# The first half of an output projection spread over six attention heads of a two-layer encoder

## What is computed

```python
for l in range(DEPTH):                                   # 2 layers
    u = rmsnorm(h, norm_g[l])
    p = u @ w_in[l]                                      # 1024 x 9216
    hq, hf_f, hf_b, hi, hgt, aq, ak, av, agt = jnp.split(p, split_idx, axis=-1)
    o_h = hgrn2_mixer(hq, hf_f, hf_b, hi, hgt, lbs[l], hg_norm_g[l])       # 8 heads
    o_a = diff_attention_mixer(aq, ak, av, agt, diff_lambda[l], diff_subln_g[l], l, cos, sin)
    mixed = jnp.concatenate([o_h, o_a], axis=-1)
    h = h + mixed @ w_out[l]                             # 2048 x 1024
out = rmsnorm(h, final_norm_g)[:, N_META:]
```

## Time and profile before

| what | value |
|---|---|
| median of 3 runs | 1385.91 us (1385.78 to 1386.55) |
| the profiled execution's own time | 1386.22 us |
| its span from first to last instruction | 1384.4 us |
| granted TensorE clock | 0.999 of 2.4 GHz |
| PE busy | 1369.9 us (99%) |
| DVE, ACT, POOL busy | 1046.2, 837.3, 186.0 us |

### The profile page before, as it was taken

The page is one execution under the profiler, slowest core; times in us unless marked ns, Lnnn a source line. Parts: engine busy times, 40 slices in busy tenths (PEclk is TensorE's granted clock), DMA queues, the critical chain, the costliest instruction groups (busy, mean ns, idle before and its releaser), DMA issues.

```text
span 1384.4 us, 32303 instructions
## 1 busy us (share of the span) xinstructions
PE 1369.9 (99%) x13108; PEld 1291.0 (93%) x13108; DVE 1046.2 (76%) x1765; ACT 837.3 (60%) x1802; POOL 186.0 (13%) x158
## 2 busy tenths in 40 slices
PE   9999999999999999999999999999999999999998
PEld 9999999998999999999998888888888899999987
DVE  6888887788646777877667888888886478888864
ACT  7666666666434666666555667666664456666654
POOL 1111222220000000000001122222210000000100
PEclk9999999999999999999999999999999999999999
DMA  5332322332323333333233232333323233334432
GB/s 188 117 98 93 108 85 86 108 108 78 99 71 122 101 99 100 103 90 100 70 107 108 87 106 85 108 107 108 108 82 108 85 110 107 108 107 114 114 96 76
DMA packets 76340, 140.41 MB, mean 101 GB/s; under 512 B 9504, under 2 KB 39456, under 8 KB 76192
## 3 DMA queue, kind: packets, MB, share of 16 engines
q1 hardware_dynamic: 76192, 138.35, 33.0%
HBM read 112.36 MB, written 17.30 MB: 94 GB/s over the span
## 4 chain that ended last, share of the span: by engine, by line
PE 89%; DVE 5%; ACT 2%; issue 2%; DMA 0%; SPq 0%; DVEq 0%; ACTq 0%
PE proj L1926 64%; PE far L2191 5%; PE pair L2174 3%; PE pair L2176 3%; PE far L2208 2%; PE pair L2059 1%; PE far L2193 1%; PE far L2144 1%; PE far L2145 1%; PE pair L2124 1%; DVE ops L1660 1%; PE pair L1926 1%; PE pair L2131 1%; DVE w_lo L1392 1%; PE far L2148 1%
## 5 line engine op out<-in xcount | busy, mean ns | idle before, releaser
L1926 PE MATMUL proj<-u_hi,w_hi 128*128 128x264 f32 (+1 forms) x1960 | 478.7, 312 | 1.9 <-DVE w_lo L1392 0.7
L1926 PE MATMUL proj<-u_lo,w_hi 128*128 128x264 f32 (+1 forms) x1960 | 458.2, 302 | 0.0
L1926 PE MATMUL proj<-u_hi,w_lo 128*128 128x264 f32 (+1 forms) x1960 | 458.1, 302 | 0.0
L1926 PEld LDWEIGHTS proj<-u_hi,w_hi 128*128 128x128 f32 x1960 | 314.7, 189 | 19.3 <-issue 1.4
L1926 PEld LDWEIGHTS proj<-u_hi,w_lo 128*128 128x128 f32 x1960 | 314.0, 188 | 13.6
L1926 PEld LDWEIGHTS proj<-u_lo,w_hi 128*128 128x128 f32 x1960 | 314.0, 188 | 10.6
L1392 DVE TENSOR_TENSOR w_lo<-w_raw,w_hi 128x1024 fp32r<-128x1024 f32 x178 | 221.9, 1247 | 35.9 <-ACT w_hi L952 35.8
L1200 ACT ACTIVATE decay<-pair,neg_max 128x528 f32<-128x528 f32 (+1 forms) x144 | 100.3, 697 | 203.4 <-DVE neg_max L1782 203.3
L952 ACT ACTIVATE w_hi<-w_raw 128x1024 fp32r<-128x1024 f32 x178 | 186.5, 1048 | 39.4 <-PE proj L1926 36.6
L1782 DVE TENSOR_REDUCE neg_max<-pair 128x1 f32<-128x528 f32 (+1 forms) x144 | 101.4, 704 | 90.5 <-PE pair L2176 89.3
L892 POOL TENSOR_TENSOR mix_lo<-mixed_t,mix_hi 128x528 fp32r<-128x528 f32 (+1 forms) x32 | 50.9, 1590 | 502.0 <-ACT mix_hi L1247 502.0
(11 more groups left out here) (257 smaller groups left out, 2245.7 us busy)
## 6 DMA issues: line engine op xcount, KB each, us to landing
w_raw<-w_units SPq DMA_DIRECT2D x178, 512.0 KB, 3.6
v_scratch<-blocks SPq DMA_DIRECT2D x128, 64.0 KB, 2.1
v_rows<-v_scratch SPq DMA_DIRECT2D x32, 256.0 KB, 2.9
o_scratch<-blocks SPq DMA_DIRECT2D x104, 64.0 KB, 2.7
q_stack<-gate_f SPq DMA_DIRECT2D x32, 132.0 KB, 2.4
k_stack<-k_stack SPq DMA_DIRECT2D x32, 132.0 KB, 2.4
o_rows<-o_scratch SPq DMA_DIRECT2D x14, 256.0 KB, 3.8
ops<-o_scratch SPq DMA_DIRECT2D x12, 256.0 KB, 2.6
```

Source lines behind the costliest of these rows:

```text
L1926: ins = pe.matmul(out, w, x[:, tile, cols_n], start=(k == 0 and p == 0), stop=(k == last_k and p == 2))
```

## The change

Four things are done together.

1. The eight `outA` units no longer all hang on head 8. Heads 8 to 13 feed 2, 1, 1, 2, 1 and 1 of them (`OUT_A_BEHIND`), and parts are carried over from head to head (`CARRIED`). Heads 8 to 13 now feed 41, 42, 41, 43, 42 and 43 pieces; heads 14 and 15 stay at 32 and 28.
2. Since the slots of `mix_hi` and `mix_lo` are then read until head 13's end, the outputs of heads 8 to 13 are kept unrounded in six rows of `ops` (free in the attention heads). All are rounded in head 14: ACT in steps 1 to 5 and 7, POOL as they come.
3. Head 7 also feeds the first four pieces of head 9's `aq` unit (`AHEAD`): 39 instead of 35.
4. Special offsets of head 8 (an earlier `av`, a later `ak`, an earlier `ag`, weight parts cut ahead of the step's own work) go.

```diff
+KEPT = range(HG_HEADS, HEADS - 2)
+OUT_A_BEHIND = dict(zip((c + 1 for c in KEPT), (2, 1, 1, 2, 1, 1)))
...
-        if c == HG_HEADS + 1:
-
-            units += [("outA", c, j, c - 1) for j in range(OUT_TILES)]
+        for _ in range(OUT_A_BEHIND.get(c, 0)):
+            units.append(("outA", c, sum(u[0] == "outA" for u in units), c - 1))
...
-def mix_step(c):
-
-    return HG_STEPS - 2 if c < HG_HEADS else 2 if c == HG_HEADS else gate_step(c) + 1
+def rounded(c, s):
+
+    if c == 0 or c - 1 in KEPT and c - 1 != KEPT[-1]:
+        return ()
+    own = HG_STEPS - 2 if c < HG_HEADS else 2 if c == HG_HEADS else gate_step(c) + 1
+    if c - 1 != KEPT[-1]:
+        return (c - 1,) if s == own else ()
+    if s == own:
+        return (c - 1,)
+    return KEPT[s - 1:s] if 1 <= s < len(KEPT) else ()
...
+CARRIED = dict(zip(KEPT, (3, 1, 0, 5, 3, 0)))
...
-    return min(c + 1, 3) if c < HG_HEADS - 1 else 0
+    return min(c + 1, 3) if c < HG_HEADS - 1 else CARRIED.get(c, 0)
+
+
+AHEAD = 4
...
-    return left + own[:len(own) - carried(c)]
+    ahead = own_pieces(c + 1)[:AHEAD] if c == HG_HEADS - 1 else []
+    return left + own[AHEAD if c == HG_HEADS else 0:len(own) - carried(c)] + ahead
...
-    return late_by(c, s, {"av": 0 if c == HG_HEADS else 1, "any": 0})
+    return late_by(c, s, {"av": 1, "any": 0})
...
-    wide = c == HG_HEADS
-    return late_by(c, s, {"ak": 2 if wide else 1, "ag": 2 if wide else 3, "outA": 0, "outB": 0, "any": 2})
+    return late_by(c, s, {"ak": 1, "ag": 3, "outA": 0, "outB": 0, "any": 2})
...
-            return ops[:, 0, 0, 0:SEQ]
+            return ops[:, 1, 2, 0:SEQ]
+
+        def mixed_of(c):
+
+            return ops[:, (c - KEPT[0]) // 4, (c - KEPT[0]) % 4, :] if c in KEPT else mixed_t[:, :]
...
-                pool.tensor_tensor(mix_lo[:, n % 8, ts], mixed_t[:, ts],
+                pool.tensor_tensor(mix_lo[:, n % 8, ts], mixed_of(n % HEADS)[:, ts],
...
-                    if c > 0:
-                        cut_mixed(n - 1)
+                    for m in [m for step_ in range(steps_of(c)) for m in rounded(c, step_)]:
+                        cut_mixed(l * HEADS + m)
...
-                        if s == mix_step(c) and c > 0:
-                            round_mixed(l, c - 1)
+                        for m in rounded(c, s):
+                            round_mixed(l, m)
...
-                        if c == HG_HEADS:
-                            cut_after(l, units_cut(c, s))
...
-                        if c != HG_HEADS:
-                            cut_after(l, units_cut(c, s))
+                        cut_after(l, units_cut(c, s))
```

More of the change, by code:

```diff
@@ L344, in units_followed @@
 def units_followed(c, s):
-    wide = c == HG_HEADS
-    return late_by(c, s, {"ak": 2 if wide else 1, "ag": 2 if wide else 3, "outA": 0, "outB": 0, "any": 2})
+    return late_by(c, s, {"ak": 1, "ag": 3, "outA": 0, "outB": 0, "any": 2})
 def split_turn(c, i):
-    return c == HG_HEADS or c > HG_HEADS + 1 and UNITS[i][0] == "ak"
+    return c == HG_HEADS or UNITS[i][0] == "ak"
 def turns_finished(c, s):
@@ L1246, in round_mixed @@
                 ts = tokens(l, "outA")
-                act.activation(mix_hi[:, c % 8, ts], mixed_t[:, ts], ACT.Copy).then_inc(mix_hi_ready, 1)
+                act.activation(mix_hi[:, c % 8, ts], mixed_of(c)[:, ts], ACT.Copy).then_inc(mix_hi_ready, 1)
             act.wait_ge(ones_set, 4)
@@ L1713, in gate_main @@
                 dve.wait_ge(stage_read, 3 * n + 3)
-                if n > 0:
-                    dve.wait_ge(mix_lo_ready, n)
-                out, by = mixed_t[:, N_META:T], gates[:, c % 2, N_META:T]
+                if n > 0 and c not in KEPT:
+                    dve.wait_ge(mix_lo_ready, l * HEADS + HG_HEADS if c - 1 in KEPT else n)
+                out, by = mixed_of(c)[:, N_META:T], gates[:, c % 2, N_META:T]
                 if sent_round(c):
@@ L1735, in gate_meta @@
                     dve.wait_ge(stage_read, 3 * n + 3)
-                    dve.wait_ge(mix_lo_ready, n)
                 dve.wait_ge(meta_turned, metas_turned(n) + 1)
-                dve.tensor_tensor(mixed_t[:, 0:N_META], meta[:, 0:N_META], gates[:, c % 2, 0:N_META], ALU.mult)\
+                dve.tensor_tensor(mixed_of(c)[:, 0:N_META], meta[:, 0:N_META], gates[:, c % 2, 0:N_META], ALU.mult)\
                     .then_inc(meta_mixed if last_is_main(c) else mixed, 1)
```

## The result

| kernel | median us | runs | against the kernel before |
|---|---|---|---|
| before | 1386.11 (1385.78 to 1386.55) | 4 | |
| changed | 1418.16 (1414.08 to 1419.62) | 4 | ratio 1.0226 (1.0211 to 1.0240), slower |

The prediction was 1392.8 us with a range from 1384.5 to 1398.5. The sign was right. The size was not: the change costs 32 us, where 6.9 were forecast. The profiled execution of the changed kernel took 1419.62 us, its span is 1417.8 us and its mean granted clock 0.992 (before 1384.4 us and 0.999).

The account below looks back on a forecast made before the run. The prediction took TensorE (PE), 99% busy at a granted clock of 0.999, as the bound. Its terms sum to 6.85 us on the profiled 1386.22 (1393.1); with that 0.3 above the median, 1392.8 us, range 1384.5 to 1398.5.

Parts of the forecast that it names:

- head 7, layer 0 / 1: Head 7 with 39 pieces: DVE's reordered work makes PE wait 0.9 us more in each layer.
- head 8, layer 0 / 1: Head 8 with 41 pieces instead of 96: shorter steps uncover waits, +2.35 us in layer 0, +1.9 in layer 1.
- heads 9 to 13: Heads 9 to 13 with 9 to 11 more pieces each: no step late except by under 0.1 us, 0.
- head 14, layer 0 / 1: Head 14: POOL's additional `mix_lo` hold operations of `aq`'s turn on DVE, +0.5 us in layer 0, +0.3 in layer 1.
- Its cover: Heads 9 to 13: 0.36 us spare in two-piece steps, more pieces in busier ones; if wrong, about 0.5 us per late step.
- The last wait: Head 7, layer 0, step 12: PE waits 1.85 us (was 0.3) for DVE's forward chain and the last gate.
- The sign named for it: Head 7, step 12: PE waits over 1.5 us for DVE's forward chain, behind the evacuation of `av`.
- the three steps named: Head 8, steps 0, 3 and 5: PE waits for exponentials, 1.0, 1.05 and 0.7 us in layer 0.
- the pieces fill the gaps: Rival: head 7's four pieces cover 2.9 of 3.2 us a layer, nothing late behind; 1379.3 us, weaker form 1383; chance 0.15.
- the change comes out even: Rival: head 7 even, head 8 loses only the first exponential, +0.6 to +2.5; 1386.5 to 1388.4 us; chance 0.15.
- the port decides: Rival: head 14's five additional `mix_lo` hold critical DVE operations, up to 5.7 us a layer; 1397 to 1401 us; chance 0.10.

Follow-up runs that it names:

- e1_stacks_first: Changed kernel with the four copies of the next head's stacks issued one step earlier on SP's queue, ahead of the weight loads: 1394.73 us.
- e5_first_noahead: `e1_stacks_first` with head 7 feeding its own 35 pieces again and head 8 feeding 45: 1387.43 us.
- the experiment on it: `e5_first_noahead` with head 14's roundings two steps apart (steps 1, 3, 5, 7, 9 and 11): 1387.42 us.
- e8_noahead_unfixed: Changed kernel with head 7 feeding its own 35 pieces and head 8 feeding 45, SP's queue as in the change: 1408.42 us.
- e4_before_behind: Kernel before with the copies of the next head's stacks issued behind the weight loads of their own step on SP's queue: 1449.94 us.

## Why the prediction was wrong, and what of it held

The steps of the sum, in us. The measured column is from the stalls of PE in `e1_stacks_first`, where the copies are in time, against the kernel before. They are taken from start times, which give 0.1 to 0.2 us more for a stall than the idle time in brackets.

| step of the prediction | predicted | measured |
|---|---|---|
| head 7, layer 0 / 1 | +0.9 / +0.9 | +0.9 / +0.4 |
| head 8, layer 0 / 1 | +2.35 / +1.9 | +2.3 / +1.7 |
| heads 9 to 13 | 0 | +1.3 (end of head 12) |
| head 14, layer 0 / 1 | +0.5 / +0.3 | +1.3 / +0.5 |
| sum | 6.85 | 8.4 (medians: 1394.73 - 1386.6 = 8.1) |
| SP's queue: waits for the stacks | not there | 16.2 |
| SP's queue: lower clock behind them | not there | about 7 (the rest of the 23.4 us that the one line is worth) |

**The step that failed** is "I find no step that comes late except by under 0.1 us: 0" for heads 9 to 13, with head 8's start beside it. Its cover was counted on ACT, DVE and POOL. SP's queue was not walked. The change doesn't touch a line of SP's, but its loads take their step from the same list as the cuts, and this list moved. "If that cover were wrong, each late step would cost about 0.5" was wrong as well: a late copy cost 0.3 us at one start and 2.2 to 3.7 us at the six others, as it is issued late and lands late, and behind most of them the clock fell.

**Head 7** went as walked in layer 0. The prediction put the starts of its three late products at 330.05, 336.75 and 345.35 us. In the changed kernel they are these, and answer to the earlier trace rows:

```profile
330.07 0.65 PE L2075 MATMUL pair<-q_level,qk_dec 128*32 128x64 f32 x32 [0.44 <-ACT q_level L1148]
...
336.80 0.52 PE L2133 MATMUL pair<-ident,ops 128*128 128x128 f32 x3 [1.68 <-ACT score L1117]
...
345.32 0.46 PE L2160 MATMUL far<-v_rows,score 128*128 128x128 f32 x2 [1.18 <-DVE mixed_t L1757]
```

The last wait was put at 1.85 and came as 1.35 by start times, with 0.3 more one step earlier. In layer 1 only 0.4 of the 0.9 us came. The sign named for it, over 1.5 us at step 12, was not met: the idle time there is 1.2 us in layer 0 and 0.6 in layer 1. DVE did what the order said, the evacuation of `av`, its transpose and a cut ahead of the forward chain, which answers to the earlier trace rows:

```profile
339.71 1.43 DVE L1592 TENSOR_TENSOR gate_f<-gate_f,q_stack 64x528 f32<-64x528 f32 x2
341.17 0.71 DVE L1477 TENSOR_TENSOR v_t<-proj,rms_inv 128x528 f32<-128x528 f32 x1
341.92 0.71 DVE L1488 STREAM_TRANSPOSE blocks<-v_t 128x512 f32<-128x512 f32 x1
342.55 1.19 DVE L1412 TENSOR_TENSOR w_lo<-w_raw,w_hi 128x1024 fp32r<-128x1024 f32 x1
343.65 0.28 DVE L1698 COPY state_f<-pair 128x128 f32<-128x128 f32 x1
```

Its busy time in the head and PE's, which answer to the earlier trace rows; the head now ends at 349.1:

```profile
306.60:349.09 42.49, 39.03 (x511) 37.91 (x510) 35.59 (x67) 23.93 (x52) 5.03 (x4) 1.00 0.33 96
```

**Head 8** held in size, and for the two longer waits in cause: 1.1, 1.15 and 0.4 us of waits at the three steps named in layer 0 of `e1_stacks_first`, where 1.0, 1.05 and 0.7 stood. (In the changed kernel the first is 0.3, since PE had waited for the copies just before.) The first exponential ends 4.4 us after its scores, as forecast, behind the one `w_hi` more. The late maximum of step 3 is there, behind a gate of 1.84 us and a cut, answering to the earlier trace rows:

```profile
361.02 1.84 DVE L1563 SCALAR_TENSOR_TENSOR gates<-stage 128x528 f32<-128x528 f32 x1
362.79 1.21 DVE L1412 TENSOR_TENSOR w_lo<-w_raw,w_hi 128x1024 fp32r<-128x1024 f32 x1
363.92 0.69 DVE L1801 TENSOR_REDUCE neg_max<-pair 128x1 f32<-128x528 f32 x1
```

But the prediction laid these waits on the spread of `outA`, 41 pieces in place of 96. `e5_first_noahead`, with 45, has none of them. They belong to the four pieces that head 7 took over: with them head 8's units are finished earlier, and the `w_hi`, the gate and the `w_lo` come ahead of an exponential and a maximum. "They are merely done there and not later" counted the four pieces as free; they cost 7.3 us.

**Head 14** was under-sized. One operation of `aq`'s turn was held for 1.1 us, as predicted, which answers to the earlier trace rows:

```profile
650.30 1.85 DVE L1585 TENSOR_TENSOR gate_f<-stage 128x528 f32<-128x528 f32 x1
652.07 0.70 DVE L1801 TENSOR_REDUCE neg_max<-pair 128x1 f32<-128x528 f32 x1
```

POOL beside it:

```profile
650.28 1.31 POOL L912 TENSOR_TENSOR mix_lo<-ops,mix_hi 128x528 fp32r<-128x528 f32 x1 [1.30 <-ACT mix_hi L1267]
```

The Trainium skill (SBUF — State Buffer, Who interferes with whom) says that a VectorE instruction with both inputs in SBUF contends with a GpSimd instruction that reads SBUF, and that the lock is exclusive. The rows agree: both start at 650.3, GpSimd's ends at 651.59, and DVE's takes its 0.71 and 1.14 more. The maximum behind it is late, and so are an exponential (0.9 us of wait) and the normalising behind that (0.4). The second was not counted. That it is the port alone isn't shown, as the experiment on it met another collision.

**The rivals.** That the pieces fill the gaps is refuted: head 7 gives back nothing, and taking the pieces away gains 7.3 us. That the change comes out even held in neither of its steps: with SP's queue in order the change still costs 8.1 us. That the port decides is refuted as the cause, though its 1397 to 1401 us were the nearest number. None of them had a queue in it.

## What to carry to other kernels

When a change moves work by a list of steps, walk every queue that takes its places from that list, the one that issues the DMAs above all. An instruction that waits there for a thing of no urgency held all that stood behind it here, so the transfers for which the bottleneck engine waits belong ahead of prefetches whose buffers aren't free yet. And where the steps of the chores follow from the count of pieces, moving a few pieces moves the chores as well: walk their order again in every stage that gives or takes pieces, with and without the move.

## What the runs showed of the hardware

A wait of PE can cost more than its length. Behind the waits of 3.7 and 3.0 us, PE's granted clock was 0.54 and 0.58 for 6 to 7 us. Waits of 2.2 to 2.4 us did it in some places (0.74 for 6.6 us from 1187.4 us on) and not in others (1.00 behind the starts of heads 8 and 10 in layer 1, at 1059 and 1145 us). In `e8_noahead_unfixed` the clock was 0.73 for the 6.3 us behind each of the five waits, those of 3.2 us and those of 2.2 to 2.5 us alike. So the length of the wait alone doesn't tell what it costs. The many waits of 0.3 to 1.9 us in head 7 and 8 never did it. Over the whole kernel, what is left for the clock came to 0.4 to 0.6 of the waits themselves: 7.8 us to 13.2 (`e8_noahead_unfixed` against `e5_first_noahead`), 7.2 to 16.2 (the changed kernel against `e1_stacks_first`), 17 to 46.6 in `e4_before_behind`. These are differences of medians less the waits, and not a measurement of the clock by itself.
